# Latent attention by pairs of heads: weights laid out by kind, scores over 64 + 32 rows, value products on both column halves

## What is computed

```python
def project_q(t):
    cq = rms_norm(t @ w_in[:, :QL], q_norm)
    return (cq @ w_qb).reshape(t.shape[0], t.shape[1], H, DN + DR)
def project_kv(t):
    a = t @ w_in[:, QL:]
    ckv = rms_norm(a[..., :MLA_KV_LORA], kv_norm)
    kv = (ckv @ w_kvb).reshape(t.shape[0], t.shape[1], H, DN + DV)
    return kv[..., :DN], kv[..., DN:], a[..., MLA_KV_LORA:]
q_rot = jnp.concatenate([q[..., :DN], apply_rope(q[..., DN:], cos, sin)], -1)
k = full_key(k_nope, apply_rope(k_pe, cos, sin))      # one rotated part for all heads
kc = full_key(kc_nope, kc_pe)
o = dense_attention(q_rot, q, k, v, kc, vc)           # latent queries: softmax over 256 context + 512 latent keys
oc = ctx_attention(project_q(hc), kc, vc)             # context queries: softmax over 256 context keys
```

## Time and profile before

| | us |
|---|---|
| median of 3 runs (4373.81 to 4380.89) | 4377.72 |
| the profiled execution | 4382.69 |
| its span | 4380.9 |
| PE busy | 4002.3 (91%) |
| DVE, ACT, POOL busy | 2177.7, 1410.8, 1505.4 |
| latent attention's four iterations | 2171.4 to 2670.3 of the span |

### The profile page before, as it was taken

The page is one execution under the profiler, slowest core; times in us unless marked ns, Lnnn a source line. Parts: engine busy times, 40 slices in busy tenths (PEclk is TensorE's granted clock), DMA queues, the critical chain, the costliest instruction groups (busy, mean ns, idle before and its releaser), DMA issues.

```text
span 4380.9 us, 56227 instructions
## 1 busy us (share of the span) xinstructions
PE 4002.3 (91%) x20797; PEld 3322.0 (76%) x20797; DVE 2177.7 (50%) x3571; ACT 1410.8 (32%) x1909; POOL 1505.4 (34%) x494
## 2 busy tenths in 40 slices
PE   6999979999999978999899988799968889988997
PEld 5888868888888867887767767578758878866885
DVE  6444856446443858564544334777753332234232
ACT  3322343223322343322333332242324432234332
POOL 1444323343343322444200002344436632334341
PEclk9999989999999988999999999899989999999998
DMA  5454423444443414443100002244424421211321
GB/s 181 141 160 144 138 75 117 150 143 147 138 157 104 132 46 128 134 154 96 50 11 10 19 1 71 74 128 142 122 69 143 144 73 55 62 61 59 95 89 55
DMA packets 529596, 440.04 MB, mean 100 GB/s; under 512 B 35932, under 2 KB 526829, under 8 KB 529197
## 3 DMA queue, kind: packets, MB, share of 16 engines
q1 hardware_dynamic: 529453, 438.11, 32.0%
HBM read 431.03 MB, written 2.83 MB: 99 GB/s over the span
## 4 chain that ended last, share of the span: by engine, by line
PE 71%; DVE 14%; issue 7%; ACT 4%; POOL 1%; DMA 1%; SPq 1%; DVEq 0%; ACTq 0%; POOLq 0%
PE ps_all L1781 19%; PE ps_all L1783 18%; PE ps_all L1782 18%; DVE acc L2345 3%; PE ps_all L1553 3%; PE ps_all L1534 2%; PE ps_all L1524 1%; PE ps_all L1846 1%; PE ps_all L1539 1%; DMA g_raw<-in_w_mod_dram 1%; PE ps_all L1631 1%; DVE full_t L2402 1%; POOL w_lo L770 1%; DVE prod_t L2420 1%; PE ps_all L1690 1%
## 5 line engine op out<-in xcount | busy, mean ns | idle before, releaser
L770 POOL TENSOR_TENSOR w_lo<-raw,w_hi 128x2048 fp32r<-128x2048 f32 (+4 forms) x326 | 1343.0, 4120 | 2407.6 <-ACT w_hi L1159 2304.3
L1781 PE MATMUL ps_all<-h_hi,w_hi 128*128 128x512 f32 (+1 forms) x2704 | 1072.9, 397 | 46.3 <-POOL h_lo L776 34.8
L1782 PE MATMUL ps_all<-h_lo,w_hi 128*128 128x512 f32 (+1 forms) x2704 | 1059.2, 392 | 0.0
L1783 PE MATMUL ps_all<-h_hi,w_lo 128*128 128x512 f32 (+1 forms) x2704 | 1058.7, 392 | 0.0
L1159 ACT ACTIVATE w_hi<-raw 128x2048 fp32r<-128x2048 f32 (+4 forms) x320 | 537.8, 1681 | 1595.8 <-PE ps_all L1783 1428.2
L1781 PEld LDWEIGHTS ps_all<-h_hi,w_hi 128*128 128x128 f32 x2704 | 518.4, 192 | 159.6 <-issue 30.1
L2345 DVE SCALAR_TENSOR_TENSOR acc<-g_raw,c_col,acc 128x256 f32<-128x256 f32 x1104 | 613.7, 623 | 1.7
L1783 PEld LDWEIGHTS ps_all<-h_hi,w_lo 128*128 128x128 f32 x2704 | 517.3, 191 | 107.6
L1782 PEld LDWEIGHTS ps_all<-h_lo,w_hi 128*128 128x128 f32 x2704 | 518.3, 192 | 103.1 <-issue 1.0
L1781 PE MATMUL ps_all<-hid_hi,w_hi 128*128 128x512 f32 (+1 forms) x1272 | 481.2, 378 | 26.7 <-DVE hid_lo L2423 17.8
L1782 PE MATMUL ps_all<-hid_lo,w_hi 128*128 128x512 f32 (+1 forms) x1272 | 472.7, 372 | 0.0
(11 more groups left out here) (328 smaller groups left out, 5388.6 us busy)
## 6 DMA issues: line engine op xcount, KB each, us to landing
raw<-in_w_ffn_gu_dram SPq DMA_DIRECT2D x88, 1024.0 KB, 5.0
g_raw<-in_w_mod_dram SPq DMA_DIRECT2D x72, 1024.0 KB, 5.0
raw<-in_ffn_w_in_dram SPq DMA_DIRECT2D x66, 1024.0 KB, 5.0
g_raw<-in_ada_w_dram SPq DMA_DIRECT2D x48, 1024.0 KB, 5.3
raw<-in_w_ffn_down_dram SPq DMA_DIRECT2D x32, 768.0 KB, 4.8
raw<-in_w_ffn_down_dram SPq DMA_DIRECT2D x32, 640.0 KB, 4.4
raw<-in_ffn_w_out_dram SPq DMA_DIRECT2D x24, 768.0 KB, 4.7
raw<-in_ffn_w_out_dram SPq DMA_DIRECT2D x24, 640.0 KB, 4.4
```

Of the source, the lines that this page charges most:

```text
L770: nc.gpsimd.tensor_tensor(v(w_lo), v(raw), v(w_hi).bitcast(F32), ALU.subtract).then_inc(sem["w_split_lo"], 1)
L1781: nc.tensor.matmul(o, whi, mhi, start=first, stop=False)
L1782: nc.tensor.matmul(o, whi, mlo, start=False, stop=False)
L1783: return nc.tensor.matmul(o, wlo, mhi, start=False, stop=last)
```

## The change

Weight panels are laid out by kind instead of by head. The 384 query columns are now four heads' 64 position-free columns (two column groups of 128, two heads each) and then four heads' 32 rotated ones (a third group); the key and value panel is 256 key columns and 256 value columns. Each panel of these comes in 8 DMAs of 64 or 32 columns (before: one), and the fourth panel of `mla_in` in 4 DMAs that repeat the same 32 columns. So two heads share a tile of 128 rows: `qn`, `qcn`, `kn` hold two heads' 64 rows, `qr`, `qt`, `qcr`, `kr` four heads' 32 rows. The rotation is done once for four heads, and DVE's copies of the rotated key and of `q_flat` go.

The attention part has 12 pairs, `MLA_PAIRS` (two heads g = 0, 1, the same query block). Scores are made in two pieces that add up in PSUM, 64 rows and 32 rows, alternating between the two heads. The value products of the two heads alternate between output rows 0 to 63 and 64 to 127. Buffers go by g: head 0 of a pair has banks 0 and 1, `prob` 0 and so on, head 1 has the others. So the next pair reuses what this pair used: `exps(n + 1, g)` waits for `turn(n, g)`, and `scores(n + 2)` for both exponentials of pair n + 1. Instructions on PE, DVE and ACT are reordered to fit. The stretches of removed code are left out:

```diff
+    spans = [(0, 256), (256, 512), (512, 640)]
+    def dma(i, j):
+        if j < 3:
+            return [(None, wp[:, :, spans[j][0]:spans[j][1]])]
+        return [(("cols", q * ROPE, ROPE), wp[:, :, LQ + LKV:LQ + LKV + ROPE]) for q in range(PER)]
...
+    def dma(i, j):
+        w, per, first, second = ((wq, DQ, NOPE, ROPE), (wkv, P, NOPE, HD))[j]
+        out = []
+        for h in range(PER):
+            out.append((("cols", h * first, first), w[:, :, ds(i * (PER * per) + h * per, first)]))
+            out.append((("cols", PER * first + h * second, second), w[:, :, ds(i * (PER * per) + h * per + first, second)]))
+        return out
...
+    MLA_PAIRS = [(hp, ctx, q) for hp in range(PER // 2) for ctx, n in ((0, 4), (1, 2)) for q in range(n)]
+    MLA_LAT = [2 * sum(1 for u in MLA_PAIRS[:n] if not u[1]) for n in range(len(MLA_PAIRS))]
...
+        act.wait_ge(sem["q_mm"], base_of("q_mm", 2) + 1)
+        nc.scalar.activation(qr[:, :], ps_all[:, 2, :], ACT.Copy).then_inc(sem["q_out"], 1)
+        act.wait_ge(sem["q_mm"], base_of("q_mm", 2) + 2)
+        nc.scalar.activation(qn[:, :, :], ps_all[:, 0:2, :], ACT.Copy).then_inc(sem["q_out"], 1)
         act.wait_ge(sem["panel_used"], st["p0"] + i * 2 + 1)
...
+        nc.scalar.activation(qcn.rearrange("p c n -> p (c n)"), ps_all[:, 3, :], ACT.Copy)
+        nc.scalar.activation(qcr[:, :], ps_all[:, 4, 0:C], ACT.Copy).then_inc(sem["q_out"], 1)
         split_hi(ahead(st, i, 0, last))
...
+        act.wait_ge(sem["key_mm"], base_of("key_mm", 2) + 1)
+        nc.scalar.activation(kn[:, :, C:T], ps_all[:, 6:8, :], ACT.Copy).then_inc(sem["kv_out"], 1)
+        act.wait_ge(sem["key_mm"], base_of("key_mm", 2) + 2)
+        nc.scalar.activation(kn[:, :, 0:C], ps_all[:, 4, :].rearrange("p (c n) -> p c n", c=2), ACT.Copy).then_inc(sem["kv_out"], 1)
+        act.wait_ge(sem["val_mm"], base_of("val_mm", 1) + 1)
+        nc.scalar.activation(vals[:, 2:6, :], ps_all[:, 0:2, :].rearrange("p b (t n) -> p (b t) n", t=2), ACT.Copy).then_inc(sem["kv_out"], 1)
+        act.wait_ge(sem["panel_used"], st["p0"] + i * 2 + 2)
+        nc.scalar.activation(vals[:, 0:2, :], ps_all[:, 5, :].rearrange("p (t n) -> p t n", t=2), ACT.Copy).then_inc(sem["kv_out"], 1)
+        def exps(n, g):
+            hp, ctx, q = MLA_PAIRS[n]
+            act.wait_ge(sem["s_max"], base_of("s_max", U) + 2 * n + g + 1)
+            if n >= 1:
+                act.wait_ge(sem["turned0"], base_of("turned0", U) + 2 * n + g - 1)
+                if not MLA_PAIRS[n - 1][1]:
+                    act.wait_ge(sem["turned1"], base_of("turned1", LU) + MLA_LAT[n - 1] + g + 1)
+            pair = ps_all[:, 2 * g:2 * g + 2, :].rearrange("p b n -> p (b n)")
...
+            nc.scalar.activation(prob[:, g, 0:W], pair[:, C:C + W], ACT.Exp, scale=DQ ** -0.5,
+                                 bias=stat[:, 4 * g + 1:4 * g + 2], accum_out=stat[:, 4 * g + 2:4 * g + 3]).then_inc(sem["s_exp"], 1)
+        def copy(n, g):
+            hp, ctx, q = MLA_PAIRS[n]
+            act.wait_ge(sem["turned0"], base_of("turned0", U) + 2 * n + g + 1)
+            if n >= 1:
+                act.wait_ge(sem["s_weighted"], base_of("s_weighted", len(MLA_PAIRS)) + n)
+            W = (2 if ctx else 3) * P
+            nc.scalar.activation(prob_t[:, g, 0:W], ps_all[:, 4, 0:W], ACT.Copy).then_inc(sem["copied0"], 1)
...
+        for g in range(2):
+            exps(0, g)
         split_hi(ahead(st, i, 1, last))
...
+        for n in range(len(MLA_PAIRS)):
+            for g in range(2):
+                if n + 1 < len(MLA_PAIRS):
+                    exps(n + 1, g)
+                copy(n, g)
+            if n >= 1 and MLA_PAIRS[n - 1][1:] in ((0, 3), (1, 1)):
+                keep(n - 1)
...
+        def queries(o, c, s):
+            cc = slice(c * P, (c + 1) * P)
             for k in range(3):
...
+                ins = triple(o, whi[:, k, cc], wlo[:, k, cc], *lows(k, s), k == 0, k == 2)
+            return ins
+        queries(ps_all[:, 2, :], 2, lat).then_inc(sem["q_mm"], 1)
+        for c in range(2):
+            ins = queries(ps_all[:, c, :], c, lat)
+        ins.then_inc(sem["q_mm"], 1)
+        for c in range(2):
+            queries(ps_all[:, 3, c * C:(c + 1) * C], c, ctx_s)
+        queries(ps_all[:, 4, 0:C], 2, ctx_s).then_inc(sem["panel_used"], 1)
+        pe.wait_ge(sem["q_out"], base_of("q_out", 3) + 1)
+        nc.tensor.matmul(ps_all[:, 5, :], turn_m[:, :], qr[:, :], start=True, stop=True).then_inc(sem["rot_mm"], 1)
...
+        for c in range(2):
+            ins = keys_of(ps_all[:, 6 + c, :], c, lat)
+        ins.then_inc(sem["key_mm"], 1)
+        pe.wait_ge(sem["q_out"], base_of("q_out", 3) + 3)
+        for c in range(2):
+            ins = keys_of(ps_all[:, 4, c * C:(c + 1) * C], c, ctx_s)
+        ins.then_inc(sem["key_mm"], 1)
...
+                vh, vl = (w[:, k, 2 * P:4 * P] for w in (whi, wlo))
...
+        for t in (2, 3, 4, 5):
+            ins = tile_of_values(ps_all[:, t // 2 - 1, (t % 2) * C:(t % 2 + 1) * C], t)
+        ins.then_inc(sem["val_mm"], 1)
+        pe.wait_ge(sem["q_rot"], base_of("q_rot", 1) + 1)
+        for t in (0, 1):
+            ins = tile_of_values(ps_all[:, 5, t * C:(t + 1) * C], t)
         ins.then_inc(sem["panel_used"], 1)
...
+        pe.wait_ge(sem["kv_out"], base_of("kv_out", 4) + 3)
         def scores(n):
...
+            hp, ctx, q = MLA_PAIRS[n]
+            if n >= 1:
+                pe.wait_ge(sem["s_exp"], base_of("s_exp", U) + 2 * n)
...
+            low_rows = lambda g: slice(g * NOPE, (g + 1) * NOPE)
+            rope_rows = lambda g: slice((2 * hp + g) * ROPE, (2 * hp + g + 1) * ROPE)
+            first, second = (lambda g: ps_all[:, 2 * g, C:2 * C]), (lambda g: ps_all[:, 2 * g + 1, :])
             if ctx:
...
+                for g in range(2):
+                    nc.tensor.matmul(first(g), qcn[low_rows(g), hp, qq], kn[low_rows(g), hp, 0:C], start=True, stop=False)
+                for g in range(2):
+                    ins = nc.tensor.matmul(first(g), qcr[rope_rows(g), qq], kr[rope_rows(g), 0:C], start=False, stop=True)
             else:
...
+                for g in range(2):
+                    nc.tensor.matmul(second(g), qn[low_rows(g), hp, qq], kn[low_rows(g), hp, C:T], start=True, stop=False)
+                for g in range(2):
+                    nc.tensor.matmul(first(g), qn[low_rows(g), hp, qq], kn[low_rows(g), hp, 0:C], start=True, stop=False)
+                for g in range(2):
+                    nc.tensor.matmul(second(g), qt[rope_rows(g), qq], kr[rope_rows(g), C:T], start=False, stop=True)
+                for g in range(2):
+                    ins = nc.tensor.matmul(first(g), qr[rope_rows(g), qq], kr[rope_rows(g), 0:C], start=False, stop=True)
             ins.then_inc(sem["s_made"], 1)
...
+        def turn(n, g):
+            hp, ctx, q = MLA_PAIRS[n]
+            u = 2 * n + g
+            pe.wait_ge(sem["s_shared"], base_of("s_shared", U) + u + 1)
+            pe.wait_ge(sem["copied0"], base_of("copied0", U) + u)
             for t in range(2 if ctx else 3):
...
+                ins = nc.tensor.matmul(ps_all[:, 4, t * P:(t + 1) * P], prob[:, g, t * P:(t + 1) * P], diag[:, g, :], start=True, stop=True)
             ins.then_inc(sem["turned0"], 1)
             if not ctx:
...
                 for t in range(3, 6):
...
+                    ins = nc.tensor.matmul(ps_all[:, 5, (t - 3) * P:(t - 2) * P], prob[:, g, t * P:(t + 1) * P], diag[:, g, :], start=True, stop=True)
                 ins.then_inc(sem["turned1"], 1)
         def weigh(n):
...
+            hp, ctx, q = MLA_PAIRS[n]
+            pe.wait_ge(sem["copied0"], base_of("copied0", U) + 2 * n + 2)
             if not ctx:
...
+                pe.wait_ge(sem["copied1"], base_of("copied1", LU) + MLA_LAT[n] + 2)
...
             for t in range(2 if ctx else 6):
...
+                for g in range(2):
+                    h = 2 * hp + g
+                    ins = nc.tensor.matmul(ps_all[g * HD:(g + 1) * HD, 6 + ctx, q * P:(q + 1) * P], vals[:, t, h * HD:(h + 1) * HD], prob_t[:, g, t * P:(t + 1) * P],
+                                           start=(t == 0), stop=(t == (1 if ctx else 5)))
             ins.then_inc(sem["s_weighted"], 1)
         scores(0)
...
+        for n in range(len(MLA_PAIRS)):
+            if n + 1 < len(MLA_PAIRS):
                 scores(n + 1)
...
+            if n == 0:
+                pe.wait_ge(sem["kv_out"], base_of("kv_out", 4) + 4)
+            else:
                 weigh(n - 1)
...
+            for g in range(2):
+                turn(n, g)
+        weigh(len(MLA_PAIRS) - 1)
...
+        rope(dve, ch, qt[:, :], qr[:, :], ps_all[:, 5, :]).then_inc(sem["q_rot"], 1)
+        def most(n, g):
+            hp, ctx, q = MLA_PAIRS[n]
+            dve.wait_ge(sem["s_made"], base_of("s_made", len(MLA_PAIRS)) + n + 1)
+            pair = ps_all[:, 2 * g:2 * g + 2, :].rearrange("p b n -> p (b n)")
+            s_ = lambda t: stat[:, 4 * g + t:4 * g + t + 1]
...
+        def copy(n, g):
```

(39 more changed lines are left out.)

219 lines of the change are left out of this document (52 added, 167 removed).

## The result

The changed kernel takes 4418.41 us in the median of its runs (4408.10 to 4432.42), the kernel before 4378.95 beside it: a ratio of 1.0094, 95% interval 1.0064 to 1.0124. It is slower by 39 us where +10 was forecast. Run once more later (experiment 1) it gave 1.0079, interval 1.0060 to 1.0098. One execution of the whole study, the profiled one of experiment 6, took 7882.67 us and is left out of that kernel's ratio.

The account below looks back on a forecast made before the run. PE was taken to bound the kernel's attention part. An iteration was 121.8 + 1.7 + 3.4 = 126.9 us for 122.6: three gave +12.9, the last -3.3, together +9.6, forecast 4387 us, range 4362 to 4428.

Parts of the forecast that it names:

- The front part: Query, key and value passes and the swap before attention: 18.8 us for 35.4, with the waits gone.
- PE's passes: Attention part: scores take 2.98 us until values start, values 1.45; 32-row products run side by side.
- Rival 3: Attention scores: 32-row products don't run side by side, 12 us an iteration, +48: 4435 us; chance 0.08.
- The chain: Long attention rounds: exponentials and copy between transposes and scores make PE wait; 10.17 us a round against 8.56.
- The attention part at full clock: Attention rounds, last transposes and values without clock falls: 103.0 us an iteration for 87.2.
- The clock: Attention holes on PE: one fall at the first, two in seven later places, 1.7 us each per iteration.
- the 3.60: A hole of 3.60 us on PE in the kernel before; the granted clock behind it went down.
- The last iteration: Fourth iteration of the step: DVE work no longer stretched beside POOL, 126.9 us for 130.2, so -3.3.
- rival 2: Attention part: the clock falls in most long rounds, +36 us more: 4423 us; chance 0.15.
- the 1.40: A hole of 1.40 us on PE in the kernel before that left the clock at full speed.
- rival 4: Front gain against attention loss: off by 2 us an iteration through hand-overs, 4379 or 4395; within the forecast's 0.55.
- Rival 1: Attention part: the clock holds and the last iteration loses its stretched waits, 4367 to 4374 us; chance 0.22.

Follow-up runs that it names:

- experiment 6: Changed kernel with each weight panel loaded in one piece in place of eight by kind: 4417.19 us, ratio 1.0089.
- experiment 2: Changed kernel with ACT's copy of a turned head put ahead of the next pair's exponential: 4342.47 us, ratio 0.9922.
- experiment 7: Changed kernel with a second set of buffers for probabilities and diagonals, ACT's order kept: 4309.72 us, ratio 0.9853.
- experiment 3: Changed kernel with idle products filling PE's holes, none in one middle pair: 4394.16 us, ratio 1.0042.
- experiment 12: Changed kernel with second probability, diagonal and turned-probability buffers, value products between transposes, one late value tile, eight idle products in the first hole: 4284.34 us, ratio 0.9781.

## Why the prediction was right and wrong

**The front part: right.** 18.8 forecast, 19.01 measured, no wait for the rotated queries. The loads hide (experiment 6).

**PE's passes: right.** Scores to values 2.98 forecast, 2.98 measured (2202.55 to 2205.53); values 1.45, measured 1.46 (to 2206.99). The 32-row products were the step without a row of their own. They run side by side: the four passes of 512 columns in 32 rows take the time of those in 64 rows, 0.97 (2204.04 to 2205.01) and 0.96. Rival 3 is out. The Trainium skill ("TensorE: Matmul & The Clock Gate", Part 3: Packing small matmuls) has 32-row products in distinct row groups overlapping; by the 0.97 the trace agrees.

**The chain: right.** A long round was forecast at 10.17 and is 10.26; the 0.09 is the copy's hand-over, 0.62 from its start to the next transposes for 0.53. Experiments 2 and 7 take out one link and then both: 8.79 and 7.64. My way from the front part's end to `scores(1)`, 6.5, is 6.38.

**The attention part at full clock: 1.6 us short.** 103.0 forecast. Each round at its full-speed length (8.79 for the first, from experiment 3, the others from iteration 2) gives 104.6, and experiment 3 ran it in 104.85. Long rounds make up 0.4 of the difference; the rest lies in rounds with short pairs (7.69 for 7.6, 5.99 for 5.7, 7.61 for 7.4) and the tail. Four iterations: 6 us, and another 1 for the four front parts.

**The clock: the mechanism right, its price wrong.** This is the step that failed: "I take a fall in two of its seven places in an iteration, 1.7 each". I took the price of a fall from one of the kernel before, behind the 3.60. The measured ones: behind the first hole 11.73 us to the next scores (2326.64 to 2338.37) for 8.79, so 2.9, not 1.7; in iterations 1, 3 and 4 it is 4.0, 3.2 and 1.5. In the rounds one fall in three of the four iterations, fewer than my two, but that of iteration 3 took 7.7 us, and those of iterations 1 and 4 took 6.3 each. I had also looked for them between long pairs; they began behind the context pairs. Why a fall lasts so much longer there isn't shown. A reading: in the kernel before PE had dense work behind a hole, and the clock was back after it, while here the half-speed round has the same holes (1.08 and 1.14 stand before its scores too), and at 1.2 GHz the engine meets the next one before it is back at 2.4. For it speaks that in experiments 7 and 12, whose long rounds have no holes ahead of the scores, a fall at the same place cost 1.7 us (a round of 8.95 for 7.30). Against it, rounds with these holes follow the first hole too, and the fall there ends within one. Sum over the four attention parts, against 104.6 each: 11.1 + 2.9 + 10.9 + 9.5 = 34.4 us, for 20.4 forecast (4 x 5.1), and two front parts at 0.87 and 0.89 another 4.8, for none. (About 1 of the 9.5 is work: the last iteration is that much longer at full clock too.) Clock 39.2 for 20.4, sums 7 too low: the step was forecast at 507.6 and measured at 533.3, and these two make up the difference. Experiment 3 shows that 32 us of it are the clock's and no work's.

**The last iteration: nearly right.** The stretched waits of before are gone, as forecast; experiment 3 leaves 1.0 us of them (105.83 for 104.85).

**The rivals.** What happened is rival 2, with 0.15: time 4423 forecast, 4418 measured. Its price of 3.1, from the 7 us at 0.53 (3.3 by the same reckoning as my 1.7), is less than half of what a fall in a round took, and it wanted four places for one; the two errors nearly cancel, so that its 4423 is luck. I chose the lower of my two rows for the forecast because the holes, 1.55 and 1.08, are each near to the 1.40 that had left the clock alone; taken together, at 2.84, they are above the 2.22 and not between, as I wrote. What the sums missed, 7 us, is the size of rival 4, and it adds to the clock's part. That the total stayed inside my range is owed to its width, since the middle missed by 31 us. Rival 1 needed less than one fall in an iteration; there were two in three of them.

**What to carry over.** When buffers are regrouped so that two units share what one had, follow the in-order queue of each engine through one round before counting passes: here the copies queued behind an exponential cost more than all the passes saved, and the swap of two lines gives it back. Price a hole on TensorE by the place it stands in: behind the first hole of an iteration a fall cost 1.5 to 4.0 us here, behind the short pairs 6.3 to 7.7, the better part of a round, and 1.7 where the long rounds had no holes (experiments 7 and 12). And look for falls where the pairs are short and the waits close together, not where the single hole is longest. An order, too, that is best with one set of buffers (copy first) can be the worse with two.
